# Small mixer products set one by one between the rows of a projection piece (mLSTM head step and gMLP transposes)

## What is computed

```python
hn = _rmsnorm(x, p['norm_pre_mix'])
z = jnp.einsum('btd,dp->btp', hn, p['w_in'])            # all mixers' inputs and 4 gate blocks
y_a = _rglru_branch(...)   # mixer A
y_b = _gmlp_branch(...)    # mixer B
y_c = _rwkv7_branch(...)   # mixer C
y_d = _mlstm_branch(...)   # mixer D
br = jnp.einsum('btnc,ncd->btnd', stack(y_a, y_b, y_c, y_d), p['w_branch'])
merged = jnp.sum(jax.nn.sigmoid(z_gate) * br, axis=2)
x = x + _rmsnorm(merged @ p['w_out'], p['norm_post_mix'])
x = x + _rmsnorm((jax.nn.silu(g) * u) @ p['w_ff_out'], p['norm_post_ffn'])   # g, u = rmsnorm(x) @ w_ff_in
```

## Time and profile before

| what | value |
|---|---|
| median of 3 runs | 2082.67 us (2082.24 to 2082.75) |
| profiled execution, its own time | 2081.98 us |
| its span | 2080.2 us |
| PE busy | 2057.8 us, 99% of the span |
| ACT, DVE, POOL busy | 765.3, 730.8, 1455.4 us |
| granted TensorE clock, mean | 0.995 |

### The profile page before, as it was taken

One profiled execution on the slowest core, in us unless ns is written; L12 is line 12 of the kernel. 1 busy time (PEld: TensorE's weight loads), 2 busy tenths in 40 slices (PEclk: granted clock), 3 DMA queues, 4 the chain that ended last, 5 costly groups with the idle time before them and its releaser, 6 DMA issues.

```text
span 2080.2 us, 39888 instructions
## 1 busy us (share of the span) xinstructions
PE 2057.8 (99%) x15931; PEld 2017.6 (97%) x15931; DVE 730.8 (35%) x1118; ACT 765.3 (37%) x939; POOL 1455.4 (70%) x1104
## 2 busy tenths in 40 slices
PE   9999999999999999999999999999999999999997
PEld 8999999999999999999999999999999999999997
DVE  5667644578333323656413511111000111111112
ACT  6354343444422222333335533333333333333332
POOL 7787756569765554678876777777777777777774
PEclk9999999999999999999999999999999999999999
DMA  7655655555544443477643444444444444444542
GB/s 255 208 173 191 197 167 186 187 171 167 165 149 136 137 130 114 131 266 248 225 155 122 153 152 151 142 156 144 151 149 149 149 151 150 149 145 145 154 151 96
DMA packets 124399, 338.90 MB, mean 163 GB/s; under 512 B 14964, under 2 KB 51428, under 8 KB 123912
## 3 DMA queue, kind: packets, MB, share of 16 engines
q1 hardware_dynamic: 106416, 315.73, 47.4%
q10 hardware_dynamic: 17880, 21.70, 2.9%
HBM read 313.50 MB, written 23.89 MB: 162 GB/s over the span
## 4 chain that ended last, share of the span: by engine, by line
PE 55%; POOL 25%; issue 19%; DVE 0%; POOLq 0%; ACT 0%; DVEq 0%
POOL w_lo L1479 25%; PE banks_g L1509 16%; PE banks_g L1510 16%; PE banks_g L1508 16%; PE banks_g L1658 1%; PE banks_m L1658 1%; PE banks_g L1660 1%; PE banks_m L1660 1%; PE banks_g L1659 1%; PE banks_m L1659 1%; PE banks_g L1686 0%; PE banks_g L1687 0%; PE banks_g L1690 0%; PE banks_m L1510 0%; PE banks_m L1509 0%
## 5 line engine op out<-in xcount | busy, mean ns | idle before, releaser
L1479 POOL TENSOR_TENSOR w_lo<-w_raw,w_hi 128x512 fp32r<-128x512 f32 (+1 forms) x1096 | 1449.1, 1347 | 604.5 <-ACT w_hi L1950 283.0
L1508 PE MATMUL banks_g<-x_hi,w_hi 128*128 128x320 f32 x3136 | 983.2, 314 | 0.3 <-ACT arena L880 0.3
L1509 PE MATMUL banks_g<-x_lo,w_hi 128*128 128x320 f32 x3136 | 970.8, 310 | 0.3 <-issue 0.3
L1510 PE MATMUL banks_g<-x_hi,w_lo 128*128 128x320 f32 x3136 | 970.8, 310 | 0.0
L1508 PEld LDWEIGHTS banks_g<-x_hi,w_hi 128*128 128x128 f32 x3136 | 590.3, 188 | 8.2 <-issue 2.4
L1509 PEld LDWEIGHTS banks_g<-x_lo,w_hi 128*128 128x128 f32 x3136 | 590.5, 188 | 2.2 <-issue 0.6
L1510 PEld LDWEIGHTS banks_g<-x_hi,w_lo 128*128 128x128 f32 x3136 | 590.3, 188 | 0.0
L1950 ACT ACTIVATE w_hi<-w_raw 128x1024 fp32r<-128x1024 f32 x196 | 206.1, 1058 | 435.6 <-PE banks_g L1510 376.8
L1831 ACT ACTIVATE w_hi<-w_raw 128x1024 fp32r<-128x1024 f32 (+1 forms) x240 | 249.7, 1041 | 240.3 <-PE banks_g L1510 239.0
L1510 PE MATMUL banks_g<-a_hi,w_lo 128*128 128x320 f32 x704 | 217.5, 309 | 0.0
L1508 PE MATMUL banks_g<-a_hi,w_hi 128*128 128x320 f32 x704 | 217.5, 309 | 0.0
(11 more groups left out here) (385 smaller groups left out, 1868.5 us busy)
## 6 DMA issues: line engine op xcount, KB each, us to landing
w_raw<-in_w_f SPq DMA_DIRECT2D x211, 512.0 KB, 3.8
w_raw<-in_w_fi SPq DMA_DIRECT2D x176, 512.0 KB, 3.6
w_raw<-in_w_fo SPq DMA_DIRECT2D x64, 512.0 KB, 3.5
front_scratch<-ev ACTq DMA_DIRECT2D x106, 160.0 KB, 2.9
w_raw<-in_w_br SPq DMA_DIRECT2D x32, 512.0 KB, 4.5
w_raw<-in_w_o SPq DMA_DIRECT2D x32, 512.0 KB, 3.6
arena<-front_scratch SPq DMA_DIRECT2D x25, 640.0 KB, 5.6
w_raw<-in_w_fo SPq DMA_DIRECT2D x32, 384.0 KB, 3.0
```

The costliest lines, as they stand in the source:

```text
L1479: low = nc.gpsimd.tensor_tensor(w_lo[:, q % RING, c0:c1], w_raw[:, q % RING, c0:c1], w_hi[:, q % RING, c0:c1].bitcast(F32), ALU.subtract)
L1508: pe.matmul(out, wh, hi[:, k0 + k, :], start=first and k == 0, stop=False)
L1509: pe.matmul(out, wh, lo[:, k0 + k, :], start=False, stop=False)
L1510: mm = pe.matmul(out, wl, hi[:, k0 + k, :], start=False, stop=last and k == tiles - 1)
```

## The change

In each D head the five steps of the first part are set between the eight rows of one more piece: query, row, key, row, then each of three tiles of key by tokens followed by a row, then each of three transposes of the value followed by a row. In B the piece that stood behind the transposes is run by rows among them: four transposes, row, two, row, two, row, two, row, two, row, and then three rows. Each head now takes 10 pieces instead of 9, so four pieces of the front move ahead of the end of D; the number of pieces is the same, 212. No small product and no wait is added or taken away.

```diff
             fill("B_v", 3)
             pe.wait_ge(S("B_v"), C4)
+            row = piece_rows()
             for t, (t0, n) in enumerate(((0, P), (P, P), (TP, 64))):
                 o = bank("B_turned", t)
                 for c in range(C4):
                     mm = pe.transpose(o[0:n, c * P:(c + 1) * P], b_v[:, c, t0:t0 + n], ident)
-                filled(mm, "B_turned", t)
-            fill("B_tok", 1)
+                    if c == 3:
+                        filled(mm, "B_turned", t)
+                    if c % 2 and (t, c) != (0, 1):
+                        next(row)
+            for _ in range(3):
+                next(row)
             for t in range(3):
                 was_read(pe, "B_turned", t)
...
                 pe.wait_ge(S("D_v_in"), 16)
+                row = piece_rows()
                 single(d_wq, d_c[:, h, :], "D_q", h)
+                next(row)
                 single(d_wk, d_c[:, h, :], "D_k", h)
+                next(row)
                 o = bank("D_ktok", h)
                 for t, (t0, n) in enumerate(token_tiles):
                     mm = pe.matmul(o[0:n, t * P:(t + 1) * P], d_c[:, h, t0:t0 + n], d_wk, start=True, stop=True,
                                    skip_group_check=True)
-                filled(mm, "D_ktok", h)
+                    if t == 2:
+                        filled(mm, "D_ktok", h)
+                    next(row)
                 o = bank("D_vtok", h)
                 for t, (t0, n) in enumerate(token_tiles):
                     mm = pe.transpose(o[0:n, t * P:(t + 1) * P], d_v[:, h, t0:t0 + n], ident)
-                filled(mm, "D_vtok", h)
+                    if t == 2:
+                        filled(mm, "D_vtok", h)
+                    next(row)
 
                 fill(("D_qk_", h), 1)
```

## The result

| what | before | after |
|---|---|---|
| median of 8 runs, interleaved | 2082.07 us (2080.46 to 2082.75) | 2088.95 us (2087.22 to 2093.3) |
| profiled execution, its own time | 2081.98 us | 2089.24 us |
| its span | 2080.2 us | 2087.4 us |
| PE busy | 2057.8 us | 2059.2 us |
| granted TensorE clock, mean | 0.995 | 0.994 |

The ratio after to before is 1.0036, with a 95% interval of 1.0028 to 1.0045: slower by over 0.2%, at almost the forecast time (2089.1).

The account below looks back on a forecast made before the run. TensorE, busy 2057.8 of 2080.2 us, was taken to bound the kernel. Terms 0.2 + 0.1 + 0 + 4.6 + 1.5 = 6.4 us on 2081.98 gave 2088.4, plus 0.7 to the median 2089.1; range 2084.6 to 2092.4.

Parts of the forecast that it names:

- The end of the front: Front's end into branch stage: four pieces fewer release SyncE later; the wait at piece 216 grows by 4.6 us.
- The clock: Behind the wait ahead of piece 216: 3 us at half the clock lose 1.5 us, bounds 0.5 and 2.
- Part 1: First step of each D head: about 2.4 us set singly, no gain, 0.04 us lost per head, 0.2 us in all.
- the rival that lived on it: The rival Single products pay: switches to a transpose drain TensorE, 2091.4 us; chance 0.09.
- Part 2: gMLP transposes in B: the 3.0 us wait ahead of them stays; cost 0.1 us, bounds 0 and 0.75.
- the slow stretch in C is shed: Rival in C: half clock at 815 to 820 us disappears, worth 2.5 to 3 us, about 2086.3 us; chance 0.08.
- Part 3, cost 0: Waits inside the D heads: the 0.3 us of each head stays, later weight loads do no harm; cost 0.
- The covered end: Rival at piece 216: its weights land within 2.9 us, the 4.6 us is made up, 2083.0 us; chance 0.15.
- The wait grows, the clock stays: Rival at piece 216: the wait grows 4.6 us with no slow clock behind it, 2087.6 us; chance 0.14.
- Single products pay: Rival in D and B: all switches to a transpose drain, 1.8 + 0.75 us in place of 0.3, 2091.4; chance 0.09.
- the change does what it says: Rival: weight loads hidden (1.2 us gained), four 0.3 us waits go, end covered, 2080.3 us; chance 0.04.

Follow-up runs that it names:

- e11: Changed kernel with weights of branch pieces 216 and 217 loaded ahead of SyncE's wait, plus 59 instructions at TensorE's program start: 2091.04 us, ratio 1.0042.
- e12: Kernel before with weights of pieces 216 and 217 loaded ahead of SyncE's wait, plus 197 instructions at TensorE's program start: 2111.27 us, ratio 1.0146.
- e8: Kernel before with the C state scaling and store later and weights of pieces 216 and 217 ahead of SyncE's wait: 2081.18 us, ratio 0.9992.
- e9: Kernel before with one edit, weights of branch pieces 216 and 217 loaded ahead of SyncE's wait for the front's stores: 2081.26 us, ratio 0.9994.
- e1: Kernel before with only the gMLP part of the change, heads as before: 2082.22 us, ratio 0.9997.
- e2: Changed kernel with one piece fewer ahead of each head's first step, so 9 pieces a head, small products still single: 2083.02 us, ratio 0.9997.
- e10: Changed kernel with 9 pieces a head and weights of pieces 216 and 217 loaded ahead of SyncE's wait: 2081.40 us, ratio 0.9998.
- e5: Changed kernel with weights of branch pieces 216 and 217 loaded ahead of SyncE's wait for the front's last stores: 2083.39 us, ratio 1.0004.

## Why the prediction was right, point by point

**The end of the front** carried the forecast, and its steps came as they were worked out. SyncE released at t = 908.51 - 894.42 = 14.1 (forecast 14.5, lower bound 14.2); three sigmoids and stores in a row behind `out_Ss`; from the release to piece 216 12.27 us (12.3 forecast, the same chain as before); piece 216 late by 5.49 us (5.9); the wait grown by 4.2 us (4.6). One sign was named too high: the row of the wait says 4.8 us, where 5 to 6 were announced. The term was 0.4 us too large, since I let the stores wait for `out_Ss`. It lands 3.9 us after its issue here, not 5.1:

```profile
out_Ss<-arena ACTq DMA_DIRECT2D x1, 1024.0 KB, 3.9
```

The last store is issued at 906.68 and SyncE goes on 1.83 us later, as before (1.84). The Trainium skill (DMA: Bandwidth & Descriptors, Queues, rings and completion order) made that 0.3 us less, and the number agrees. But `out_Ss` had landed by 906.9, before the last store could, so no row here shows a store that passes it. The three stores themselves land at 907.3, 907.8 and 908.5, each behind it and in order.

**The clock** was the term mis-sized: 1.5 us forecast, 2.5 measured. I took 3 us at half the clock from the stretch behind the gMLP wait. The stretch here lasts 919.5 to 926.3, of which 5.5 us fall on products. The trace of before had a longer one, too, around 815 to 820; it lasts 6.8 us (813.5 to 820.3), and my upper bound should have been half of that, 3.4, not 2.

**Part 1** held: the first step of head 0 costs 284.10 - 278.02 - 25 x 0.1467 = 2.41 us above its rows (2.4 forecast). The query set singly costs 0.54 us there, as it did in the group, so hiding its weight load brought nothing. Some of its rows:

```profile
278.02 0.31 PE L1522 MATMUL banks_g<-x_hi,w_lo 128*128 128x320 f32 x1
278.16 0.70 PE L401 MATMUL banks_m<-arena 128*128 128x320 f32 x2
...
281.29 0.31 PE L1643 MATMUL banks_g<-x_hi,w_lo 128*128 128x320 f32 x1
281.53 0.43 PE L468 MATMUL banks_m<-arena 128*64 128x128 f32 x2
281.89 0.42 PE L1641 MATMUL banks_g<-x_hi,w_hi 128*128 128x320 f32 x1
...
283.40 0.31 PE L1643 MATMUL banks_g<-x_hi,w_lo 128*128 128x320 f32 x1
283.55 0.27 PE L475 MATMUL banks_m<-con,arena 128*64 128x128 f32 x1
283.57 0.39 PE L1641 MATMUL banks_g<-x_hi,w_hi 128*128 128x320 f32 x1
283.81 0.31 PE L1642 MATMUL banks_g<-x_lo,w_hi 128*128 128x320 f32 x1
284.10 0.31 PE L1520 MATMUL banks_g<-x_hi,w_hi 128*128 128x320 f32 x1
```

The tile of 64 tokens (281.29 to 282.15 for L1642) costs 0.57 us, the transpose of 64 tokens (283.40 to 283.81) 0.11 us, as the other two do. So the drain of 0.15 us at a transpose between rows does not exist here, and the rival that lived on it falls. By the Trainium skill (TensorEngine Tiling (Array Packing), Key Properties) the 64-token transpose should have paid as the 64-token product does; the trace does not agree for the transpose, and does for the fp32 product, 0.57 against the 0.22 us of a tile of 128 tokens.

**Part 2** was 0.1 us forecast. The stretch from the gMLP wait on came 0.4 us late, and all of it is the wait, 3.5 against 3.0 us. That wait is 3.0 to 4.0 us in the twelve kernels, shifted or not, so the difference more likely belongs to the execution than to the change.

**What the prediction had no step for** is the stall in C, 2.1 us. It left the trace's sum almost right because other things in C gave as much back. Followed at the same small products of both traces, pieces counted out, the changed kernel is 0.6 us late at the end of D, 0.1 ahead of the stall, 2.3 behind it, 0.8 where the low clock of the kernel before ends and 0.5 at the end of C. So the clock gave back 1.5 us: it was low for 3.4 us (830.8 to 834.2) and not 6.8 (813.5 to 820.3). The rest came back where two small waits of the kernel before are gone, 0.6 us at the start of C (the short stall described under e11 and e12) and 0.3 at L688. That is about half of the rival "the slow stretch in C is shed", at the same time, and it is luck: among the nine-piece kernels that stretch is 6.8 us long in before, e8 and e9 and absent in e1, e2 and e10, so it differs by several us from one execution to the next where nothing is shifted.

**Luck in the number.** The forecast of 2089.1 was 6.4 us for the trace and 0.7 us from the trace to the median. The trace showed 7.3 us, 0.9 more (the clock term 1.0 too small, the wait 0.4 too large, 0.5 ahead of the branch stage where 0.3 was forecast), and the median then lay 0.3 us under the profiled execution and not 0.7 above it. The two errors cancel; that 2088.95 is 0.15 us from the forecast says nothing of how well the terms were sized. The mechanism of the main term, and its size to 0.4 us, are what came true.

**What the stall leaves in the medians.** The changed kernel lies 6.9 us above the kernel before beside it and e10, with all small products singly, no branch wait and no stall, 1.0 us under its own: 7.9 us between them (the same from the ratios). The branch stage alone loses 8.07 us in the trace, so nothing is left over for the stall. e5, where the branch stage is cured and the stall stands, lies 1.5 us over e10 in the same way (1.2 by the ratios), 0.57 of it the branch stage; intervals of 0.0018 do not tell the remaining 1 us from 0 or from 2. "Part 3, cost 0" was true for the waits that it went through, and it looked only at data.

**The rivals.** The covered end falls: piece 216's weights took 7.2 us to land (7.5 before), not under 3. "The wait grows, the clock stays" falls with the 0.50 at 919.6 to 926.2, though e1 shows that it was a real possibility (below). "Single products pay" and "the change does what it says" fall with the 0.2 us of the four heads and with their unchanged 0.3 us waits.

## What to carry to other kernels

Work that covers a chain at a stage's end is spent when pieces are moved ahead of it, so count that chain against what remains before anything is moved; and put a transfer that does not need a wait ahead of it in its queue, since e5 took back nearly the whole loss with three lines. Where an engine shows "issue" among tiny instructions, move only the code (some idle instructions in front) before looking for a cause in the data. Single placement of small fp32 products between large ones gained nothing here and cost 0.2 us in four heads: a product of 320 columns took 0.54 us in the group and singly.

## What the runs showed of the hardware that was not expected

- **A stall that depends on where the code lies.** 2.1 to 2.8 us at one place of the program, moved away by 59 instructions and brought about by 197 (one trace each), with a shorter one of 0.2 to 0.6 us at another place that comes and goes the opposite way. Each of the fourteen traces has one of the two, and it ends 2.2 to 2.5 us after the start of a 16 KB transfer of instructions.
- **The same idleness does not always lower the clock.** e1 waits 3.6 us ahead of the gMLP transposes, longer than before's 3.0, and stays at 1.00 behind it, where the kernel before has 0.50:

```profile
170.40:174.00 3.60, 2.75 (x21) 2.69 (x22) 1.20 (x2) 1.20 (x2) 1.94 (x2) 1.00 0.71 165
```

  Its span is 2076.2 us and its median 2082.22; its eleven runs reach from 2078.0 to 2085.8 us. Its trace is 4.0 us shorter than that of the kernel before. Nearly all of this goes at two places where the kernel before has the low clock and it has not: 1.6 us behind the gMLP wait and 2.9 us in C. So single executions of one kernel can differ by several us through the clock. Two profiled executions should not be compared by their spans before these stretches are set apart.
- **VectorE beside GpSimd.** The four `y_lo` products take 3.73 us where GpSimd splits weights beside them for 2.6 us, and 5.9 to 6.0 where it does all along. That is an estimate of 1.5 us for one beside a split; the rest of the 3.73 us leaves about 0.5 us for one alone.
